# Five of seven input projections a layer as three products of rounded parts; an expert's 128-slot job in pieces of 1024

## What is computed

```python
h = x
for i in range(2):
    z = rmsnorm(h, norm_mix[i]) @ w_in[i]      # 1024 -> 2616 columns, split below
    # a_q a_k a_v a_g a_lr: gated linear attention | b_u: causal pools
    # c_q c_k c_v c_qi c_ki c_wi: top-64 sparse attention | d_uv: chunked gMLP (512 columns)
    h = h + concat([gla(...), pool(b_u), dsa(...), sgu(d_uv)]) @ w_out[i]
    h = h + cross_attn(rmsnorm(h, norm_xa[i]), mem, ...)
    hn = rmsnorm(h, norm_ffn[i])
    h = h + (swiglu(hn, ...) if i == 0 else moe_swiglu(hn, router, w1, w3, w2))  # top 2 of 8
return rmsnorm(h, final_norm)
```

## Time and profile before

| | |
|---|---|
| median of three runs | 1341.15 us |
| the profiled execution | 1340.37 us, span 1338.6 us |
| TensorE busy | 1253.7 us (94%) |
| VectorE, ScalarE, GpSimd busy | 495.1, 371.4, 85.0 us |
| DMA, mean over the span | 326 GB/s, 435.79 MB |
| mean granted TensorE clock | 0.991 |

### The profile page before, as it was taken

The page is one execution under the profiler, slowest core; times in us unless marked ns, Lnnn a source line. Parts: engine busy times, 40 slices in busy tenths (PEclk is TensorE's granted clock), DMA queues, the critical chain, the costliest instruction groups (busy, mean ns, idle before and its releaser), DMA issues.

```text
span 1338.6 us, 15258 instructions
## 1 busy us (share of the span) xinstructions
PE 1253.7 (94%) x6128; PEld 757.9 (57%) x6128; DVE 495.1 (37%) x846; ACT 371.4 (28%) x563; POOL 85.0 (6%) x69
## 2 busy tenths in 40 slices
PE   8999999999999999999989889889779999999876
PEld 6868888888887787334333224224226788434222
DVE  2746487777653826201001001001007987101002
ACT  2532454444324413101001001001006775101002
POOL 0570000000007300000000000000000000000000
PEclk9999999999999999999999999999999999999999
DMA  9733515442463078899999999999999999899996
GB/s 345 313 124 122 209 61 223 185 157 83 161 282 123 33 289 355 344 436 425 433 427 435 427 437 426 437 426 433 433 427 427 427 427 389 369 429 426 428 428 262
DMA packets 32648, 435.79 MB, mean 326 GB/s; under 512 B 5260, under 2 KB 7376, under 8 KB 9296
## 3 DMA queue, kind: packets, MB, share of 16 engines
q1 hardware_dynamic: 32400, 434.48, 78.2%
q0 software_dynamic: 192, 0.53, 0.1%
HBM read 433.94 MB, written 1.05 MB: 325 GB/s over the span
## 4 chain that ended last, share of the span: by engine, by line
PE 66%; DMA 29%; DVE 2%; ACT 1%; SPq 1%; issue 1%; DVEq 0%
DMA ring<-in_experts 28%; PE bank L2240 13%; PE bank L2334 9%; PE bank L1720 7%; PE bank L2248 6%; PE bank L2117 6%; PE bank L1725 5%; PE bank L1746 4%; PE bank L2121 3%; PE bank L2002 1%; PE bank L2009 1%; PE bank L2003 1%; PE bank L2192 1%; PE bank L2167 1%; DMA ring<-in_packed 1%; ACT r L900 1%
## 5 line engine op out<-in xcount | busy, mean ns | idle before, releaser
L2240 PE MATMUL bank<-ring,xs 128*64 128x512 f32 x1568 | 360.4, 603 | 40.0 <-DMA ring<-in_experts 39.8
L2240 PEld LDWEIGHTS bank<-ring,xs 128*64 128x64 f32 x1568 | 111.6, 138 | 250.1 <-issue 216.3
L1590 DVE TENSOR_TENSOR s_act<-wsT,bank 128x256 f32<-128x256 f32 x49 | 20.6, 421 | 505.0 <-ACT wsT L982 505.0
L2248 PE MATMUL bank<-ring,s_act 128*64 128x512 f32 x736 | 171.7, 606 | 26.8 <-DMA ring<-in_experts 26.7
L2248 PEld LDWEIGHTS bank<-ring,s_act 128*64 128x64 f32 x736 | 53.6, 139 | 131.5 <-issue 118.8
L2117 PE MATMUL bank<-x_both,wf_hi 128*128 128x512 f32 x336 | 118.9, 396 | 0.0
L982 ACT ACTIVATE wsT<-bank 128x256 f32<-128x256 f32 x49 | 18.8, 383 | 330.9 <-PE bank L2192 330.9
L1614 DVE TENSOR_TENSOR ring_lo<-ring,w_hi 128x2048 fp32r<-128x2048 f32 (+1 forms) x44 | 95.9, 2192 | 15.8 <-ACT w_hi L1040 15.7
L916 ACT ACTIVATE wf_hi<-ring 128x1024 fp32r<-128x1024 f32 x66 | 69.7, 1060 | 96.9 <-PE bank L2117 66.1
L1720 PE MATMUL bank<-xnT,ring 128*128 128x256 f32 (+1 forms) x416 | 92.5, 380 | 2.9 <-DVE xnT L1159 1.1
L2121 PE MATMUL bank<-x_both,wf_lo 128*128 128x256 f32 x336 | 94.2, 280 | 0.0
(11 more groups left out here) (379 smaller groups left out, 1445.7 us busy)
## 6 DMA issues: line engine op xcount, KB each, us to landing
ring<-in_experts SPq DMA_DIRECT2D x93, 2048.0 KB, 18.8
ring<-in_experts SPq DMA_DIRECT2D x36, 4096.0 KB, 25.9
ring<-in_packed SPq DMA_DIRECT2D x18, 1536.0 KB, 6.8
ring<-in_packed SPq DMA_DIRECT2D x11, 2048.0 KB, 13.0
ring<-in_packed SPq DMA_DIRECT2D x18, 1024.0 KB, 4.9
extra<-in_experts SPq DMA_DIRECT2D x3, 2048.0 KB, 9.7
ring<-in_packed SPq DMA_DIRECT2D x2, 656.0 KB, 7.1
ring<-in_packed SPq DMA_DIRECT2D x1, 1312.0 KB, 5.5
```

The source lines that it names most:

```text
L2240: i = mm(ps[d % 2][SMALL * side:SMALL * side + SMALL, :], xs[:, k, :], weights(u)[:, at:at + FC], start=k == 0, stop=k == KT - 1)
L2248: i = mm(ps[6 + half][SMALL * side:SMALL * side + SMALL, :], s_act[:, d % 4, x + side, :], weights(UNIT_OF["out", d, 0])[:, at:at + FC], s ...
```

## The change

**Input projections.** AG, CV, BU, CQ and UV become three products of rounded parts each, in this order after `logit`; QI and A stay as they are. x is rounded in two token halves, `x_hi` (over the tiles of memory keys and values, and of uvg) and `x_lo` (in place over xnT). ScalarE makes all `hi`, GpSimd all `lo`. The units get other slots: QI 3, CQ 4, CV 5, BU 6, A 0, AG 1, UV 2. CQ's and UV's `hi` go to the freed slots of QI and A, the others' to the upper half of their own slot. The order of loading stays QI, A, AG, CQ, CV, BU, UV; the quarters of the output projection are loaded in the order 2, 3, 0, 1.

**Moved.** The scaling of the memory weights goes from GpSimd to VectorE, where it stands with the split of row 2 ahead of q's copy. GpSimd scales memT behind the subtractions in layer 0, clears r2 behind bu's (layer 0) or cq's (layer 1), and subtracts rows 0 and 1 behind the pools. ScalarE copies rows 0 and 1 between uv1's and uv0's copies. UV is made for tile 1 first. The GLA masks come after CQ, and `logit` ahead of AG.

**Full job.** Pieces of 1024 everywhere, `lo` in a tile `w_lo` of its own, and SyncE waits for the last piece's `lo_ready` of a unit rather than for TensorE.

```diff
-PIECE, NB = 2048, 4
+PIECE, NB = 1024, 4
-        for cut in (((0, 1024), (1024, 2048), (2048, 4096)) if u < 2 else ((0, 2048), (2048, 4096)))]
+        for cut in ((0, 1024), (1024, 2048), (2048, 3072), (3072, 4096))]
-U_A, U_AG, U_CQ, U_CV, U_BU, U_QI, U_UV = SLOTS
+U_QI, U_CQ, U_CV, U_BU, U_A, U_AG, U_UV = SLOTS
+HI_OF = {U_CQ: U_QI, U_UV: U_A}
...
+        HI_ORDER = [("ag", "x1", "x0", "cv", "bu", "cq0", "cq1", "uv0", "uv1", "row2", "row3", "row0", "row1", "row4"),
+                    ("ag", "cv", "bu", "cq0", "cq1", "x1", "x0", "uv0", "uv1", "row2", "row3", "row0", "row1", "row4")]
...
@@ sync @@
-                for i in range(4):
+                for i in (2, 3, 0, 1):
+                    if i == 0:
+                        sp.wait_ge(slot_free[U_CQ], turn[1])
                     unit(1, U_WOUT + i, ring[:, U_WOUT + i, 0:2048], packed("wout", layer, i))
+                sp.wait_ge(slot_free[U_UV], turn[1])
...
-                        sp.wait_ge(slot_free[slot], 1)
-                        sp.wait_ge(slot_free[slot], turns[t])
+                        if pieces is None:
+                            sp.wait_ge(slot_free[slot], 1)
+                            sp.wait_ge(slot_free[slot], turns[t])
+                        else:
+                            sp.wait_ge(S["lo_ready"], pieces + (LAST[(u - RING) % len(JOB_UNITS)] + 1))
...
@@ gpsimd @@
+                def lo_of(*parts):
+                    for part in parts:
+                        gp.wait_ge(S["hi_done"], hi_count(layer, part))
+                        if part[0] == "x":
+                            t = int(part[1])
+                            gp.wait_ge(slot_free[U_A], first_ended)
+                            i = gp.tensor_tensor(x_lo[t], x_raw[t], x_hi[:, t, :, :], ALU.subtract)
...
+                            i = gp.tensor_tensor(part_lo(part), part_raw(part), part_hi(part), ALU.subtract)
+                        i.then_inc(S["lo_done"], 1)
+                def room():
+                    gp.wait_ge(S["scored"], second)
+                    take_wait()
+                    gp.memset(r2[:, :], 0.0).then_inc(S["r2_zero"], 1)
...
+                if layer < 1:
+                    lo_of("ag", "x1", "x0", "cv", "bu")
+                    room()
+                    lo_of("cq0", "cq1", "uv0", "uv1")
+                    gp.wait_ge(S["xT_a"], count(0, 2, 2, 2))
+                    gp.tensor_tensor(memT[:, :, :], memT[:, :, :], rs_mem.unsqueeze(1).broadcast_to([P, KT, MEM]), ALU.mult)\
+                      .then_inc(S["xT_v"], 2)
+                else:
+                    lo_of("ag", "cv", "bu", "cq0", "x1", "x0", "cq1")
+                    room()
+                    lo_of("uv0", "uv1")
                 gp.wait_ge(g_ev["bu"], L1)
...
+                lo_of("row0", "row1")
@@ scalar @@
+                if layer:
+                    hi_of("ag", "cv", "bu")
                 group("ki")
...
                 out_of("a", gla[:, 0:512], ps[6][:, :])
+                if layer < 1:
+                    act.wait_ge(S["zeroed"], 2)
+                    hi_of("ag", "x1")
+                else:
+                    hi_of("cq0", "cq1", "x1", "x0")
                 out_of("av", av[:, :, :], v3(ps[7], 0, 512, 2))
...
+                    hi_of("x0")
...
+                if layer < 1:
+                    hi_of("cv", "bu")
+                else:
+                    hi_of("uv0", "uv1")
                 out_of("ag", sg[:, :, :], v3(ps[5], 0, 512, 2), ACT.Silu)
+                if layer < 1:
+                    hi_of("cq0", "cq1", "uv0", "uv1")
...
+                out_of("bu", bu[:, :, PAD:PAD + SEQ], v3(ps[2], 0, 512, 2))
+                rows_split(2)
+                rows_split(3)
                 out_of("k", kT[:, :, :], v3(ps[4], 0, 512, 2))
...
+                out_of("uv1", uvg[:, 1, :], ps[7][:, :], ACT.Gelu_apprx_tanh)
+                rows_split(0)
+                rows_split(1)
+                out_of("uv0", uvg[:, 0, :], ps[4][:, :], ACT.Gelu_apprx_tanh)
@@ vector @@
+                out_of("cv", cv[:, :, :], v3(ps[3], 0, 512, 2))
+                dve.wait_ge(arrived[U_WKV], layer * (16 * LAYER_TURNS) + 32)
+                for k in range(KT):
+                    w = ring[:, U_WKV, 512 * k:512 * k + 512]
+                    i = dve.tensor_scalar(w, w, pcol[layer][:, R_MEM + k:R_MEM + k + 1], None, mult)
+                i.then_inc(S["wkv_scaled"], 1)
+                rows_split(2)
                 out_of("q", qT[:, :, :], v3(ps[7], 0, 512, 2))
-                out_of("cv", cv[:, :, :], v3(ps[5], 0, 512, 2))
+                rows_split(3)
...
-                dve.tensor_tensor(ring_lo[slot][:, lo:hi], ring[:, slot, lo:hi],
+                dve.tensor_tensor(w_lo[:, i % NB, 0:hi - lo], ring[:, slot, lo:hi],
@@ tensor @@
+                def tokens(dst, xs_, w, t, opens=False, closes=False):
+                    for k in range(KT):
+                        i = mm(dst, xs_[:, k, :], w[:, k, :], start=opens and k == 0, stop=closes and k == KT - 1,
+                               skip_group_check=True)
+                    return i
...
+                for t in (1, 0):
+                    hi_ready(f"x{t}")
+                    tokens(side(5, t), x_hi[:, t, :, :], wh, t, opens=t == 1)
+                    lo_ready("ag")
+                    tokens(side(5, t), x_hi[:, t, :, :], wl, t)
+                for t in (1, 0):
+                    lo_ready(f"x{t}")
+                    i = tokens(side(5, t), x_lo[t], wh, t, closes=True)
+                i.then_inc(g_ps["ag"], 1)
...
+                wh, wl = unit_parts(U_UV)
+                hi_ready("uv1")
+                for t, bank, name in ((1, 7, "q"), (0, 4, "k")):
+                    pe.wait_ge(g_ev[name], L1)
+                    tokens(ps[bank][:, :], x_hi[:, t, :, :], wh, t, opens=True)
+                    tokens(ps[bank][:, :], x_lo[t], wh, t)
+                lo_ready("uv1")
+                for t, bank in ((1, 7), (0, 4)):
+                    i = tokens(ps[bank][:, :], x_hi[:, t, :, :], wl, t, closes=True)
+                    i.then_inc(g_ps[f"uv{t}"], 1)
```

More of the change, by code:

```diff
@@ L697, in _ @@
                 first, second = (layer * 2 + 1), (layer * 2 + 2)
-                landed1 = (layer * (16 * LAYER_TURNS) + 32)
+                first_ended = (layer * LAYER_TURNS + 2)
                 restart()
-                gp.wait_ge(S["scored"], second)
-                take_wait()
-                gp.memset(r2[:, :], 0.0).then_inc(S["r2_zero"], 1)
-                for t in (bu, pw1, pw2):
-                    link(gp.memset(t[:, :, 0:PAD], 0.0))
-                gp.wait_ge(arrived[U_WKV], landed1)
@@ new lines, in hi_ready, with lo_ready, side @@
+                def hi_ready(part):
+                    pe.wait_ge(S["hi_done"], hi_count(layer, part))
+                def lo_ready(part):
+                    pe.wait_ge(S["lo_done"], lo_count(layer, part))
+                def side(bank, n):
+                    return ps[bank][:, 256 * n:256 * n + 256]
+                wh, wl = unit_parts(U_AG)
+                hi_ready("ag")
+                for t in (1, 0):
[3 more added lines that the diff above has]
+                    tokens(side(5, t), x_hi[:, t, :, :], wl, t)
@@ new lines, in _ @@
+                for t in (1, 0):
+                    lo_ready(f"x{t}")
+                    i = tokens(side(5, t), x_lo[t], wh, t, closes=True)
+                i.then_inc(g_ps["ag"], 1)
+                wh, wl = unit_parts(U_CV)
+                hi_ready("cv")
+                pe.wait_ge(S["rel"], second)
+                for t in range(TT):
+                    tokens(side(3, t), x_hi[:, t, :, :], wh, t, opens=t == 0)
+                    tokens(side(3, t), x_lo[t], wh, t)
+                lo_ready("cv")
@@ new lines, in _ @@
+                i.then_inc(g_ps["bu"], 1)
+                pe.wait_ge(g_ev["av"], L1)
+                wh, wl = unit_parts(U_CQ)
+                hi_ready("cq1")
+                for m in range(4):
+                    features(side((7, 4)[m // 2], m % 2), wh[:, :, P * m:P * m + P], opens=m % 2 == 0)
+                    features(side((7, 4)[m // 2], m % 2), wh[:, :, P * m:P * m + P], lo=True)
+                lo_ready("cq1")
+                for m in range(4):
+                    i = features(side((7, 4)[m // 2], m % 2), wl[:, :, P * m:P * m + P], closes=True)
+                    if m == 1:
+                        i.then_inc(g_ps["q"], 1)
@@ L1919, in _ @@
                 pe.wait_ge(S["xT_v"], count(0, 2, 2, 2))
-                pe.wait_ge(S["wkv_scaled"], lo_of_rows(layer, 0) - 1)
-                pe.wait_ge(g_ev["uv0"], L1)
+                pe.wait_ge(S["wkv_scaled"], L1)
+                pe.wait_ge(g_ev["uv1"], L1)
                 w = v3(ring[:, U_WKV, :], 0, 4096, KT)
@@ L1953, in _ @@
                 pe.wait_ge(S["p"], first)
-                pe.wait_ge(g_ev["uv1"], L1)
+                pe.wait_ge(g_ev["uv0"], L1)
                 for hh in range(HEADS):
@@ L2314, in piece @@
```

(12 more changed lines are left out.)

200 lines of the change are left out of this document (111 added, 89 removed).

## The result

The changed kernel took 1375.49 us in the median of four runs (1372.11 to 1375.80), the kernel before 1341.19: a ratio of 1.0247, 95% interval 1.0235 to 1.0260. It is 34 us slower by the medians. I had forecast 1359, in a range from 1334 to 1370: the direction was right, the size was not.

A forecast was written before the change was run, and what follows sets the result against it. Bound: TensorE's chain in the trunk, which shifts the DMA-bound expert part one for one. 1341.15 + 17.6 (layer 0) + 4.7 (layer 1) - 3.4 (full job) = 1360.0, taken as 1359 us; range 1334 to 1370.

The forecast's parts named there:

- the meetings: VectorE steps in both layers wait for whole GpSimd subtractions, up to 4.5 us each; layer 0 +17.6 us, layer 1 +4.7.
- Rivals A and B: VectorE against GpSimd: no meeting matters, 1323 us, 1 in 10; or holds are short, 1344 to 1351 us, 2 in 10.
- 1348 us for the shortest hold: Whole kernel's time if each GpSimd subtraction held VectorE only 0.85 us, layer 0 losing 9.6 us and layer 1 0.
- Gaps of 13 and 7 us on TensorE in layer 0 may cost a few us at half clock; I add nothing, the range holds it: TensorE idling in layer 0 may slow its clock afterwards; a few us possible, none added to the forecast.
- the sum: Whole kernel: 1341.15 + 17.6 (layer 0) + 4.7 (layer 1) - 3.4 (full job) = 1360.0, then taken as 1359 us.
- the walk: Step-by-step schedule of both layers with whole GpSimd holds: layer 0 +17.6 us, layer 1 +4.7.
- a late copy: ScalarE copies uv0 after rows 0 and 1, delaying LayerNorm and the logits: 2.2 us in layer 0, 2.4 in layer 1.
- Rival C: VectorE's memory-weight scalings also use GpSimd's side and alternate with pooling steps: +6.4 us a layer, 1372 us, 0.6 in 10.
- 0.41 us for 256 columns is full price: Evidence that VectorE's scalings do not use GpSimd's side: the threshold step with plain constants takes 0.29 us.
- the full job: Earlier freed slots at the job's end give back 3.4 us, 0 to 6; it stays TensorE-bound at 126 us.
- TensorE's own gain: Rounded products in the input projections take 39.5 us a layer instead of 48.5, gaining 9.0 us a layer.

The follow-up runs named there:

- Experiment 4: The changed kernel with GpSimd's subtractions for the input projections replaced by memsets about as long that read no tensor: 1348.66 us, ratio 1.0048.
- the usual execution: The changed kernel run again, nothing altered, for its spread and a second profile: median 1375.47 us, profiled execution 1375.45; seven of eight took 1373.4 to 1377.4.
- experiment 1: The changed kernel with TensorE kept busy in its gaps of both mixing stages by products nothing reads: 1363.56 us, ratio 1.0172.
- experiment 6: The changed kernel with GpSimd's subtractions waiting for VectorE's scores, logit bias and decay steps: 1369.29 us alone, 1356.93 us with q's and uv0's copies also moved first.
- the ten runs alone: The kernel before with only the full job's part of the change: 1338.42 us, ratio 0.9979, ten runs.

## Why the prediction was wrong in size

**Right: the meetings, and how long one holds.** The range turned on whether GpSimd's subtraction holds VectorE for its whole 4.5 us, where the rows showed no wait above 0.84. I took the whole one. The forecast ends of the first four held steps in layer 0 came within 0.3 us, those of tile 0's threshold and mask within 0.9 (68.1 and 72.6, forecast 68.8 and 73.5). The logit bias came at 72.64 (74.0 forecast), masks' products at 89.69 (90.4), UV at 98.94 (99.2). In layer 1, counted from its start 20.8 us late, the masks came at +4.5 us (forecast +4.9). Experiment 4 takes the reads away and leaves GpSimd as long busy: 27 us go. Rivals A and B are dead: no VectorE step of the meetings got by in less than what was left of GpSimd's instruction. (The prediction's 1348 us for the shortest hold is 1347.4 by its own terms; nothing hangs on it.) The Trainium skill, "SBUF — State Buffer", section "Who interferes with whom", says that the one which comes second is fully blocked, for the whole instruction: the trace now agrees, with 4.60 us.

**Wrong: the step "Gaps of 13 and 7 us on TensorE in layer 0 may cost a few us at half clock; I add nothing, the range holds it".** Against the usual execution (1375.45 us, trunk 38.0 us late) the sum had 22.3 for the two layers, so 15.7 are missing. The filled kernel of experiment 1 puts 6.4 of them in layer 0 (140.21 less 133.84) and 7.7 in layer 1 by the same reading (from layer 0's output projection to the first expert load it took 360.65 us against 368.33), together 14.0; by the medians of the two kernels it is 12 us. The gaps were in the walk, 13 and 7 us long. The earlier trace rows has only a mean of 0.97 where TensorE idled, but the trace of before shows what is behind such a mean, the 16 products behind a wait, the next 16, and the clock of a stretch among the first:

```profile
676.06 5.35 PE L2240 MATMUL bank<-ring,xs 128*64 128x512 f32 x16 [2.17 <-DMA ring<-in_experts]
...
681.93 3.65 PE L2240 MATMUL bank<-ring,xs 128*64 128x512 f32 x16
```
```profile
677.00:680.00 3.00, 3.00 (x10) 1.21 (x8) 0.00 (x0) 0.00 (x0) 0.00 (x0) 0.50 1.01 437
```

I priced the gaps' length and not what follows them. In layer 1 I did not look at all: there the clock cost as much as in layer 0, most of it in the stretch of small products behind UV, where the walk had only 2.4 us for a late copy.

**The other 1.7 us** are a balance. In the filled kernel the stretch from UV's end to the output projection (layer 0) or the first expert load (layer 1) is 3.5 us longer than in the kernel before, in each layer, where the walk had 2.2 and 2.4; UV of layer 0 ended 0.9 us ahead of the walk. In that stretch GpSimd's rows 0 and 1, which the change put behind the pools, meet the step on the variances and the negation of the maxima in each layer (layer 1 of the changed kernel):

```profile
473.48 2.13 DVE L1183 TENSOR_SCALAR st<-st 128x2 f32<-128x2 f32 x1
...
478.41 1.68 DVE L1349 TENSOR_SCALAR st<-st 128x4 f32<-128x4 f32 x1
```

2.13 and 1.68 us where such a step takes 0.17. No run takes these two meetings away alone, so that they are the 2.4 us is argued from these rows. I had walked the meetings up to UV and taken the chain behind UV from the kernel before, though the rows' subtractions had moved into it.

**Rival C, the scalings on VectorE,** gave about the measured time (1372), and that is luck. The scalings do use GpSimd's side: 0.47 us is the shortest of one, 0.78 the mean of eight beside pooling steps, so the meetings cost 2.4 us a layer and not 6.4, and the eight took 6.2 us where the sum had 5.4. Their real price shows only where the long GpSimd instructions fall on them, 16.6 us in experiment 6. My evidence against C, "0.41 us for 256 columns is full price", was no evidence: it was one row, of a step of another form.

**Right: the full job.** 3.4 us forecast, 3.0 by the traces, 2.6 by the ten runs alone. It stayed bound by TensorE (124.7 us).

**Right, and of no use: TensorE's own gain.** 9.0 us a layer were forecast from rows, and with the copies first and GpSimd standing back UV does end 2 us earlier in layer 0 and 9 earlier in layer 1. What the kernel as changed did with it was to wait.

## What to carry to other kernels

When long two-input subtractions are added on GpSimd, walk VectorE's whole list beside them, not only where they are wanted: in these traces every VectorE step with two tensors in SBUF, or with one and constants, waited for the whole of the GpSimd subtraction ahead of it. Making GpSimd wait does not remove a meeting, it moves it to the next thing on VectorE's list; it is removed by giving one of the two jobs to ScalarE (8.6 us here) or by letting VectorE do the subtraction itself in 2.3 us instead of being held for 4.6 (7.7 us, part of it the clock behind).

Every gap on TensorE that a forecast finds has to be priced twice, for its length and for the half clock behind it: here 12 to 14 of 34 us.

## What the runs showed of the hardware that I had not expected

A memset on GpSimd, which reads no tensor, left VectorE's score steps alone (0.38 us each) and yet held steps with one tensor and constants: 13.90 us for eight scalings in experiment 4, against 0.47 us for the shortest single one in any run, and 0.70 us for tile 0's threshold step, which takes 0.23 in the kernel before. MAX8 and MATCH_REPLACE8 ran at full speed beside subtractions and memsets alike (0.29 and 0.28 us). A scan of 256 columns was held like the others (4.86 us beside memT's product, 0.69 alone).

The same program falls into half clock behind layer 0's UV in one execution and not in another (1375.45 and 1372.11 us), which alone makes 3.6 us.
